# RWKV-7 recurrence: a decay constant moved into the exponentials' scale, the key's factors made on ScalarE tile by tile, and the zero padding written at the input norm

## The reference, cut to what matters

```python
xs = h[None] + xx[None] * mix[:, None, None, :]
r, k, v = ... xs[:3] @ w_in
w_log = -jax.nn.softplus(-(w0 + jnp.tanh(xw @ w1) @ w2)) - 0.5
decay = jnp.exp(-jnp.exp(w_log))
a = jax.nn.sigmoid(a0 + (xa @ a1) @ a2)
kk = heads(k * k_k);  kk = kk / norm(kk)
k = k * (1.0 + (a - 1.0) * k_a)
y = scan over tokens of  s * decay + (s @ -kk) (kk * a) + v k,  read out with r
```

## Time and profile before

| what | value |
|---|---|
| median of three runs | 2455.79 us (2455.34 to 2458.22) |
| profiled execution, its own time | 2454.03 us |
| its span | 2452.2 us |
| PE busy | 2330.4 us, 95% |
| DVE busy | 1472.2 us, 60% |
| ACT busy | 1017.9 us, 42% |
| POOL busy | 1815.1 us, 74% |

### The profile page before, as it was taken

One profiled execution on the slowest core, in us unless ns is written; L12 is line 12 of the kernel. 1 busy time (PEld: TensorE's weight loads), 2 busy tenths in 40 slices (PEclk: granted clock), 3 DMA queues, 4 the chain that ended last, 5 costly groups with the idle time before them and its releaser, 6 DMA issues.

```text
span 2452.2 us, 53546 instructions
## 1 busy us (share of the span) xinstructions
PE 2330.4 (95%) x20664; PEld 2255.9 (92%) x20664; DVE 1472.2 (60%) x1834; ACT 1017.9 (42%) x1513; POOL 1815.1 (74%) x853
## 2 busy tenths in 40 slices
PE   7999999999999899999999789999999999999998
PEld 7999989999998789999998588978999999998997
DVE  6972148945962437954981956637972893335982
ACT  4344344344343434344343543325344434444342
POOL 5887737887887627887888796837888788746886
PEclk9999999999999999999999789999999999999999
DMA  5554524564553414554555132013554555433553
GB/s 186 173 193 138 180 65 139 175 199 126 174 191 128 133 35 144 173 202 124 172 188 178 51 115 78 4 37 120 171 186 157 154 178 191 146 103 108 175 189 111
DMA packets 89949, 348.83 MB, mean 142 GB/s; under 512 B 9968, under 2 KB 11760, under 8 KB 89712
## 3 DMA queue, kind: packets, MB, share of 16 engines
q1 hardware_dynamic: 89840, 347.31, 44.5%
HBM read 346.22 MB, written 1.05 MB: 142 GB/s over the span
## 4 chain that ended last, share of the span: by engine, by line
PE 42%; DVE 23%; issue 18%; POOL 8%; ACT 7%; DVEq 1%; DMA 0%; ACTq 0%; SPq 0%; POOLq 0%
PE bank L298 10%; PE bank L300 10%; PE bank L299 10%; DVE hid_hi L1494 9%; DVE hid L1492 7%; POOL w_lo L1269 5%; PE bank L630 3%; ACT sg L983 3%; DVE gs L1435 3%; PE bank L361 2%; PE bank L363 2%; PE bank L362 2%; DVE hid_lo L1496 2%; ACT w_hi L887 1%; POOL h L1282 1%
## 5 line engine op out<-in xcount | busy, mean ns | idle before, releaser
L1269 POOL TENSOR_TENSOR w_lo<-raw,w_hi 128x1024 fp32r<-128x1024 f32 (+2 forms) x608 | 1606.9, 2667 | 554.0 <-ACT w_hi L887 533.7
L298 PE MATMUL bank<-x_hi,w_hi 128*128 128x272 f32 (+1 forms) x3312 | 974.9, 294 | 33.5 <-POOL x_lo L1295 14.9
L300 PE MATMUL bank<-x_hi,w_lo 128*128 128x272 f32 (+1 forms) x3312 | 961.5, 290 | 0.0
L299 PE MATMUL bank<-x_lo,w_hi 128*128 128x272 f32 (+1 forms) x3312 | 957.8, 289 | 0.0
L887 ACT ACTIVATE w_hi<-raw 128x1024 fp32r<-128x1024 f32 (+2 forms) x608 | 660.4, 1115 | 233.5 <-PE bank L300 212.2
L298 PEld LDWEIGHTS bank<-x_hi,w_hi 128*128 128x128 f32 x3312 | 629.7, 190 | 48.8 <-issue 25.1
L299 PEld LDWEIGHTS bank<-x_lo,w_hi 128*128 128x128 f32 x3312 | 631.5, 191 | 0.2
L300 PEld LDWEIGHTS bank<-x_hi,w_lo 128*128 128x128 f32 x3312 | 630.5, 190 | 0.0
L1496 DVE TENSOR_TENSOR hid_lo<-hid,hid_hi 128x272 f32 (+3 forms) x176 | 422.7, 2402 | 20.2
L298 PE MATMUL bank<-hid_hi,w_hi 128*128 128x272 f32 (+1 forms) x1408 | 405.1, 288 | 3.2 <-POOL w_lo L1269 3.1
L300 PE MATMUL bank<-hid_hi,w_lo 128*128 128x272 f32 (+1 forms) x1408 | 403.6, 287 | 0.0
(11 more groups left out here) (283 smaller groups left out, 2417.6 us busy)
## 6 DMA issues: line engine op xcount, KB each, us to landing
raw<-in_ffn_in SPq DMA_DIRECT2D x352, 512.0 KB, 3.5
raw<-in_ffn_out SPq DMA_DIRECT2D x128, 704.0 KB, 4.0
raw<-in_sb_in SPq DMA_DIRECT2D x48, 512.0 KB, 3.5
raw<-in_rw_in SPq DMA_DIRECT2D x24, 512.0 KB, 3.3
raw<-in_sb_out SPq DMA_DIRECT2D x16, 512.0 KB, 3.5
raw<-in_mla_out SPq DMA_DIRECT2D x8, 512.0 KB, 3.3
raw<-in_rw_lora SPq DMA_DIRECT2D x8, 512.0 KB, 4.7
raw<-in_rw_out SPq DMA_DIRECT2D x8, 512.0 KB, 3.3
```

What stands on the lines that cost most here:

```text
L298: nc.tensor.matmul(o, wh, xh[:, k, cols()], start=start, stop=False)
L299: nc.tensor.matmul(o, wh, xl[:, k, cols()], start=False, stop=False)
L300: last = nc.tensor.matmul(o, wl, xh[:, k, cols()], start=False, stop=stop)
L1269: nc.gpsimd.tensor_tensor(w_lo[:, s, w], raw[:, s, w], w_hi[:, s, w], ALU.subtract).then_inc(lo_ready, 1)
```

## The change

Four things are done, all for layer 2.

1. L1668 is gone. `w_` keeps the plain sigmoid, `cs` and `ex3` are running sums of it, and the three exponentials on ACT take the constant as their `scale` (`-DECAY`, `DECAY`, `-DECAY`, with `DECAY` = exp(-0.5)). Of `w_` itself nothing else is read before L1702 overwrites it.
2. L1673 is gone from DVE. ACT makes the same factors as eight tiles, Identity(k_a * `a_` - k_a), in a new step `key_gains` that the table `between` puts behind unit k2. It needs the column `less_ka` = -k_a, which DVE makes in one small instruction. Both the scale and the bias are columns.
3. DVE waits for the eight tiles (`key_gain_ready`) ahead of L1682.
4. The five memsets of the padding stand at the input norm, ahead of DVE's wait for the root, together with `less_ka`.

The new tensor `less_ka` has 8 columns and lies before `gains`.

```diff
+DECAY = float(np.exp(-0.5))
...
-                    nc.scalar.activation(ex3[:, :, :], ex3[:, :, :], ACT.Exp).then_inc(pprev_ready, 1)
+                    nc.scalar.activation(ex3[:, :, :], ex3[:, :, :], ACT.Exp, scale=-DECAY).then_inc(pprev_ready, 1)
...
-                    nc.scalar.activation(ex2[:, :, :], cs[:, :, :], ACT.Exp, scale=-1.0).then_inc(pinv_ready, 1)
+                    nc.scalar.activation(ex2[:, :, :], cs[:, :, :], ACT.Exp, scale=DECAY).then_inc(pinv_ready, 1)
...
-                    nc.scalar.activation(cs[:, :, :], cs[:, :, :], ACT.Exp).then_inc(pinc_ready, 1)
+                    nc.scalar.activation(cs[:, :, :], cs[:, :, :], ACT.Exp, scale=-DECAY).then_inc(pinc_ready, 1)
+                def key_gains():
+                    for b in range(4):
+                        act.wait_ge(bank_free[b], uses_at[sec_k.name_key][b] + 1)
+                    for k in range(DT_):
+                        nc.scalar.activation(ex2[:, k, :], a_[:, k, 0:L], ACT.Identity, scale=vecs[:, V_KA + k:V_KA + k + 1],
+                                             bias=less_ka[:, k:k + 1]).then_inc(key_gain_ready, 1)
-                between = {("k", 1, 0): decay_before, ("r", 0, 0): kk_squares, ("r", 0, 1): decay_inverse,
+                between = {("k", 0, 2): key_gains, ("k", 1, 0): decay_before, ("r", 0, 0): kk_squares, ("r", 0, 1): decay_inverse,
...
                 n["sq"] += DT_
+                for x in (r_, k_, w_, a_, v_):
+                    nc.vector.memset(x[:, :, L:LP], 0.0)
+                steps.link(nc.vector.tensor_scalar_mul(less_ka[:, :], vecs[:, V_KA:V_KA + DT_], -1.0))
                 inverse_root()
...
-                steps.link(nc.vector.tensor_scalar_mul(w_[:, :, 0:L], w_[:, :, 0:L], -float(np.exp(-0.5))))
...
-                steps.link(nc.vector.scalar_tensor_tensor(ex2[:, :, :], a_[:, :, 0:L], -1.0, wide(V_KA), ALU.add, ALU.mult))
-                for x in (r_, k_, w_, a_, v_):
-                    last = nc.vector.memset(x[:, :, L:LP], 0.0)
-                steps.link(last)
...
                 dve.wait_ge(kkraw_ready, 1)
+                dve.wait_ge(key_gain_ready, DT_)
```

More of the change, by code:

```diff
@@ L111, in build @@
         acc, std = sb("acc", [P, L]), sb("std", [P, L])
-        xr = sb("xr", [P, L])
+        xr, less_ka = sb("xr", [P, L]), sb("less_ka", [P, DT_])
         gains = sb("gains", [P, DEPTH * 6 * DT_])
@@ L223, in build @@
         xx_ready, xm_ready, lt_ready, lhi_ready = sem("xx_ready"), sem("xm_ready"), sem("lt_ready"), sem("lhi_ready")
-        rwc_loaded, kprime_ready = sem("rwc_loaded"), sem("kprime_ready")
+        rwc_loaded, key_gain_ready, kprime_ready = sem("rwc_loaded"), sem("key_gain_ready"), sem("kprime_ready")
         kksq_ready, kkmax_ready, kklog_ready, kkroot_ready, head_sum = (sem(n) for n in ("kksq_ready", "kkmax_ready", "kklog_ready", "kkroot_ready", "head_sum"))
```

## The result

The changed kernel takes 2504.84 us (2495.45 to 2509.78), the one before 2457.01 us (2455.34 to 2458.23) beside it: a ratio of 1.0191, 95% interval 1.0175 to 1.0207. It was forecast 2.3 us faster and is 48 us slower.

What follows compares the result with a forecast made beforehand. POOL's 2.5 us lateness before r was taken as the bound: relief of 3.29 us less a 0.6 us wait, of which 2.3 us pass PE, so 2455.79 - 2.3 = 2453.5 us; 8-in-10 range 2450.9 to 2456.4.

Steps and rivals of the forecast that it cites:

- C: Rival, section r: the clock drops, all 72 matmuls take 0.226 us, 2.3 us slower, 2458.1 us; chance 0.06.
- The alternation: Section k: POOL and DVE instructions take strict turns, so L1672 or L1673 costs POOL 2.22 us, a scan 0.45.
- The terms of the local sum: Section k to r: POOL relieved of 1.07 and 2.22 us, together 3.29, less a 0.6 us wait for ACT.
- `x_lo` of `k`: Section k: the fourth meets a scan in place of L1668, so the eighth is done 0.66 us earlier.
- `key_gains`, and POOL's wait behind it: Section k: eight ACT tiles take 4.0 us, and POOL waits 0.6 us before the w_lo of k7.
- `x_lo` of `r`: Start of section r: begins at 1440.6 in place of 1443.17, 2.6 us earlier; PE's wait falls from 3.87 to about 1.9.
- The sums over heads: End of section r: PE's results come 2.0 to 2.5 us earlier, 2.3 taken, and these sums move with them.
- B: Rival, section r: the clock stays up, 25 matmuls save 0.1 us each, 4.8 us gained in all, 2451.0 us; chance 0.11.
- 0.226: Section r: the time in us of one PE matmul at the low clock; 29 slow ones were counted after the change.
- The memsets at the input norm: Input norm: with less_ka they fit in DVE's idle 7.57 us and cost nothing; otherwise 0.4 to 1.2 us lost.
- Everything behind hangs on these results, and moves with them: Behind section r: sums over heads, roots, w_lo of v and the recurrence keep the whole 2.3 us gain.

Runs made afterwards that it cites:

- b_shift32: The kernel before with one unused tensor of 8 columns (32 bytes) where less_ka lies in the changed kernel, no instruction different: 2512.47 us, ratio 1.0225.
- a_inplace: The changed kernel with less_ka as a view of the first 8 columns of pend, so every tensor lies where it lay before: 2454.97 us, ratio 0.9995.
- a_late: a_inplace with one more DVE wait, for the last w_lo of v, ahead of the product of a_ and m: 2451.60 us, ratio 0.9977.
- a_shift64: The changed kernel with less_ka of 16 columns (64 bytes), of which 8 are used: 2455.88 us, ratio 0.9999.
- a_half: a_inplace with the key's factors left on DVE and no key_gains, keeping only the constant in the exponentials and the moved memsets: 2455.18 us, one execution.
- b_late: The kernel before with nothing but the added DVE wait of a_late: 2454.04 us, ratio 0.9993.
- b_both: b_raw32 with a gap of 16 columns, not 8, ahead of w_lo, which moves w_lo and all behind it 32 bytes further: 2507.40 us, ratio 1.0215.
- b_raw32: The kernel before with unused columns: 8 ahead of raw, 56 behind it and 8 ahead of w_lo: 2456.08 us, ratio 1.0004.
- b_head32: The kernel before with 8 unused columns behind xr and 24 behind vecs: gains, consts, cbf, vecs 32 bytes on, w_hi, w_lo 128: 2456.16 us, ratio 0.9999.

## Why the prediction was wrong

**The step that failed for the 48 us is one that the sum does not have.** The prediction priced every instruction that the change adds, removes or moves, and called the range from there. The new tensor of 8 columns, named in the text on the change, had no term. It moves all tensors behind it by 32 bytes, and `w_lo` comes to 192 of 256 bytes from `raw`. In the eight output sections, which the change does not touch, the accumulation waits for up to six `w_lo`, the one under way and five more, and 29.9 of the trace's 41.4 us go there. 12.1 more go ahead of them, where every `w_lo` is some 30 ns longer; that the longer `w_lo` is their cause is an estimate and was not tried by itself. b_shift32 shows that the 32 bytes alone cost the whole, a_inplace that without them nothing is lost. None of the rivals was near: C, the slower side, was a clock in section `r`.

**The alternation was taken for a rule.** "The times fit a strict alternation" holds for the earlier trace rows and for the accumulations (at most 3.6 us) and the large instructions of section `r` in every trace at the other distances. The Trainium skill (SBUF — State Buffer, "Who interferes with whom") says that the shared port pair is held for a whole instruction and that the loser blocks fully. The 2.07 and 18.20 us agree with that. It also says that issue order decides who blocks. For who gets the pair at the next boundary that does not hold here: the accumulation started at 730.64 us, ahead of the third `w_lo` at 732.40, and that one and four more went first. What did decide, with the same instructions in the same order, was the place of `w_lo` against `raw`; by what mechanism stays open.

**The terms of the local sum held.** They can be read in a_inplace, whose tensors lie as before; its first mixed tile is at 1351.87 us. POOL there:

```profile
1407.70 7.95 POOL L1305 TENSOR_TENSOR x_lo<-k_,x_hi 128x272 fp32r<-128x272 f32 x8
1415.61 15.26 POOL L1279 TENSOR_TENSOR w_lo<-raw,w_hi 128x1024 fp32r<-128x1024 f32 x5
1431.29 9.47 POOL L1279 TENSOR_TENSOR w_lo<-raw,w_hi 128x1024 fp32r<-128x1024 f32 x4 [0.43 <-ACT w_hi L889]
1440.72 10.22 POOL L1305 TENSOR_TENSOR x_lo<-r_,x_hi 128x272 fp32r<-128x272 f32 x8
```

- `x_lo` of `k`: 7.95 us against 8.59, 0.64 less; forecast 0.66.
- `key_gains`, and POOL's wait behind it: 4.15 and 0.43 us; taken were 4.0 and 0.6. ACT's row:

```profile
1425.84 4.15 ACT L1175 ACTIVATE ex<-a_,pend,vecs 128x272 f32<-128x272 f32 x8
```

- `x_lo` of `r` begins 88.85 us after the mixer's start, before 91.17: 2.3 us; forecast 2.6. The row of `k` itself began 0.4 us later than before; counted from there it is 2.71. PE waits 1.94 us for it; forecast 1.9:

```profile
1441.62 0.36 PE L363 MATMUL bank<-x_hi,w_hi 128*128 128x272 f32 x1 [1.94 <-POOL x_lo L1305]
1445.91 0.39 PE L363 MATMUL bank<-x_hi,w_hi 128*128 128x272 f32 x1 [1.79 <-POOL x_lo L1305]
1448.81 0.60 PE L363 MATMUL bank<-x_hi,w_hi 128*128 128x272 f32 x1 [1.89 <-POOL x_lo L1305]
```

- The sums over heads begin 108.75 us after the start, before 110.94: 2.2 us; taken was 2.3. The gaps of PE did not keep the clock up (B) nor hold it down (C) in this trace. In a_late, with the same instructions so far, the sums begin at 106.73, 4.2 us earlier than before and near B's 4.8; its clock is back at 1.00 where that of a_inplace is not. So what PE makes of POOL's lead moves by 2 us from trace to trace, and that 2.2 came out so near 2.3 is in part luck. The windows of a_late and of a_inplace, with the columns of the earlier trace rows:

```profile
1452.79:1455.79 3.00, 3.00 (x26) 3.00 (x25) 0.00 (x0) 2.63 (x3) 1.56 (x2) 1.00 0.49 150
```

```profile
1452.00:1455.00 3.00, 3.00 (x16) 3.00 (x16) 0.00 (x0) 1.02 (x2) 1.28 (x1) 0.54 0.15 40
```

- One reading was loose: at the low clock give 0.217 us for a matmul (23 in 5.00 us), the prediction took 0.226. It hardly matters, since the count before and the count after have nearly as many slow ones (25 and 29).
- The memsets at the input norm take 0.38 us each, and the eight additions to `h` 5.80 us in the changed kernel against 5.78: free, as forecast.

**The step that failed locally is "Everything behind hangs on these results, and moves with them".** `x_lo` of `v` still begins 2.2 us earlier, 126.77 against 128.97, but `tv` is copied at 160.50 against 160.27. In section `v` of a_inplace DVE and POOL show why:

```profile
1485.65 2.59 POOL L1279 TENSOR_TENSOR w_lo<-raw,w_hi 128x1024 fp32r<-128x1024 f32 x1
1489.54 17.28 POOL L1279 TENSOR_TENSOR w_lo<-raw,w_hi 128x1024 fp32r<-128x1024 f32 x4 [1.29 <-ACT w_hi L889]
```

```profile
1488.58 2.42 DVE L1711 SCALAR_TENSOR_TENSOR w_<-m,ex 128x2176 f32<-128x2176 f32 x1
1491.04 4.52 DVE L1713 TENSOR_TENSOR a_<-a_,m 128x2176 f32<-128x2176 f32 x1
```

and the kernel before:

```profile
1490.75 15.97 POOL L1269 TENSOR_TENSOR w_lo<-raw,w_hi 128x1024 fp32r<-128x1024 f32 x4 [0.18 <-ACT w_hi L887]
```

```profile
1490.90 4.52 DVE L1702 SCALAR_TENSOR_TENSOR w_<-m,ex 128x2176 f32<-128x2176 f32 x1
```

Before, the first product of DVE came 0.15 us after a `w_lo` had begun and had to wait for it (4.52 us), so that three of the four `w_lo` were held up. In a_inplace it came 0.96 us ahead of the `w_lo`, in a moment when POOL waited for ACT, ran bare (2.42 us) and held up the first one too: the four take 17.28 us and not 15.97. The other 1.1 us are POOL's wait ahead of these four, 1.29 us and not 0.18, and ACT had the same 1.1 us from PE, whose first round of `v` took longer. ACT in a_inplace, then before:

```profile
1488.11 0.40 ACT L1189 ACTIVATE v_<-bank 128x272 f32<-128x272 f32 x1 [7.63 <-PE bank L365]
```

```profile
1489.32 0.40 ACT L1179 ACTIVATE v_<-bank 128x272 f32<-128x272 f32 x1 [6.52 <-PE bank L363]
```

PE ran that round at a granted clock of 0.50 over six us, where before it rose in them (columns: busy us and count of PE, PEld, DVE, ACT, POOL; clock; DMA). a_inplace, then before:

```profile
1479.00:1482.00 3.00, 2.45 (x11) 2.48 (x12) 2.24 (x3) 1.48 (x3) 3.00 (x5) 0.50 0.63 212
1482.00:1485.00 3.00, 3.00 (x15) 3.00 (x15) 3.00 (x5) 0.00 (x0) 3.00 (x4) 0.50 0.01 3
```

```profile
1482.00:1485.00 3.00, 3.00 (x17) 3.00 (x18) 2.90 (x4) 0.81 (x1) 3.00 (x4) 0.62 0.56 182
1485.00:1488.00 3.00, 3.00 (x22) 3.00 (x21) 3.00 (x4) 0.00 (x0) 3.00 (x5) 0.81 0.00 0
```

From the first `x_lo` of `v` to `tv` it is 33.7 us in a_inplace and again in a_shift64, which has the same instructions, and 31.3 us in the kernel before, in the six others with its instructions at distances other than 192, and in a_half. So the 2.4 us are the same each time they occur. That collisions in this stretch cost time is shown by a_late and b_late, which take most of them away (28.6 and 29.1 us); the parting into 1.3 us of collision and 1.1 us of clock is read from traces, and neither was tried by itself. In a_half `x_lo` of `v` began at 126.84, as in a_inplace, and `tv` came at 158.17, so the luck of one boundary is worth about as much as the change.

## What to carry to other kernels

When a change allocates something, the moved addresses are a part of the change: compare first a stretch that the change doesn't touch, and try the kernel before with an unused tensor of the same size. Where GpSimd and VectorE share their port, count a gain as arrived only when the next stretch in which both are busy is behind it, and take the large VectorE instructions out of GpSimd's row with a wait if they have slack: that one wait, with the change, gave the fastest version here (0.9977); in the kernel before it gained nothing that its interval shows (0.9993).

## What the hardware showed that was not expected

- VectorE can be passed over by GpSimd at five boundaries in a row, 18.2 us for an instruction of 0.43, and at nine in a row in section `r` of b_both. It happens in all six kernels in which GpSimd's output `w_lo` lies at 192 of 256 bytes from its first input `raw`, and in none of the twelve others. Why this distance does it stays open, all the more as it also happens beside `x_lo`, whose own places against each other are the same in all. Distances of 96 and 128 and any off the grid of 32 bytes were not tried, nor other kernels.
- It costs 1.4% to 2.2% in this kernel, without a single changed instruction. A part of that comes without any instruction being passed over: most of the 12 to 19 us in the stretches with the input sections, where no instruction of VectorE took over 3.5 us.
- An activation with two columns as operands takes 4.15 us for eight tiles of 272, against 2.67 us with none and 3.39 us with one, near the 4.0 and 4.05 that the prediction had from less.
- From the grams to the end of the mixer the traces differ by up to 3 us with the same instructions (161.9 us in b_raw32, 165.1 us in b_head32, from the first `am` to the residual). A gain of 2 us in one stage is therefore seen by landmarks within the stage, not by the total.
